# mLSTM in four blocks of 128 tokens with a carried memory, computed with tokens on partitions inside the input projections

## The reference

```
lf = log_sigmoid(fg); bt = cumsum(lf)                       # within a chunk
dmat[t,s] = bt[t] - bt[s] + ig[s]   (s <= t)
mt  = max(max_s dmat, bt + m)
w   = exp(dmat - mt);  sqk = (q k^T / sqrt(128)) * w
num = sqk @ v + exp(bt + m - mt) * (C q);  den = sum(sqk) + exp(bt + m - mt) * (n q)
h   = num / max(|den|, exp(-mt))
C, n = decayed C, n + sum_s wk[s] v[s] k[s]^T, ... k[s]      # memory and normaliser
out_a = rms(sigmoid(o) * h) per head, then times mix_g, then W_out
```

## Time and profile before

| | |
|---|---|
| median of 3 runs | 1237.59 us |
| profiled execution, whole time | 1238.54 us |
| its span in the trace | 1236.7 us |
| TensorE busy in the span | 1164.5 us (94%) |
| VectorE / ScalarE / GpSimd busy | 534.4 / 339.7 / 128.1 us |
| granted clock of TensorE, mean | 0.943 |

### The profile page before, as it was taken

How to read it: one execution, slowest core, us unless ns; L and a number is a source line. 1 busy time by engine, 2 the same in 40 slices (tenths; PEclk the granted TensorE clock), 3 DMA queues, 4 the chain that set the end, 5 groups by cost and what they waited for, 6 DMA issues and landing times.

```text
span 1236.7 us, 21696 instructions
## 1 busy us (share of the span) xinstructions
PE 1164.5 (94%) x9019; PEld 1125.6 (91%) x9019; DVE 534.4 (43%) x820; ACT 339.7 (27%) x426; POOL 128.1 (10%) x231
## 2 busy tenths in 40 slices
PE   6899999999999789999978999889999999999994
PEld 6899999999999779989965779879999999999994
DVE  5435334333334577733743233474333343333345
ACT  5322132221323343122530001243221222212231
POOL 0000709500000006001223100000000000000000
PEclk9999999999999889999986668979999999999997
DMA  5222222332222202221500002212222222322221
GB/s 211 76 93 86 85 86 85 87 94 91 70 93 69 91 35 69 86 69 52 130 28 32 21 17 94 86 33 77 95 85 85 86 85 86 90 94 87 76 76 72
DMA packets 30475, 97.86 MB, mean 79 GB/s; under 512 B 5848, under 2 KB 6104, under 8 KB 30296
## 3 DMA queue, kind: packets, MB, share of 16 engines
q1 hardware_dynamic: 30424, 97.14, 25.0%
HBM read 92.43 MB, written 4.70 MB: 79 GB/s over the span
## 4 chain that ended last, share of the span: by engine, by line
PE 88%; DVE 7%; ACT 2%; DMA 2%; issue 1%; DVEq 0%; SPq 0%; ACTq 0%
PE ps L1471 77%; PE ps L1561 2%; PE ps L1759 1%; DVE y L852 1%; DVE x L856 1%; DMA raw<-wout 1%; PE ps L1766 1%; PE ps L1713 1%; PE ps L1540 1%; DVE xl L805 1%; DVE wl L688 1%; PE ps L1752 1%; ACT wh L402 1%; PE ps L1739 0%; DMA raw<-w 0%
## 5 line engine op out<-in xcount | busy, mean ns | idle before, releaser
L1471 PE MATMUL ps<-xh,wh 128*128 128x272 f32 x1936 | 411.8, 295 | 31.7 <-DVE xl L805 24.5
L688 DVE TENSOR_TENSOR wl<-raw,wh 128x1024 fp32r<-128x1024 f32 (+1 forms) x169 | 205.5, 1216 | 515.3 <-ACT wh L402 514.6
L1471 PE MATMUL ps<-xl,wh 128*128 128x272 f32 x1936 | 406.6, 292 | 0.0
L1471 PE MATMUL ps<-xh,wl 128*128 128x272 f32 x1936 | 404.7, 291 | 0.0
L1471 PEld LDWEIGHTS ps<-xh,wh 128*128 128x128 f32 x1936 | 309.1, 192 | 37.8 <-issue 27.6
L1471 PEld LDWEIGHTS ps<-xl,wh 128*128 128x128 f32 x1936 | 311.1, 193 | 0.0
L1471 PEld LDWEIGHTS ps<-xh,wl 128*128 128x128 f32 x1936 | 309.8, 192 | 0.0
L402 ACT CAST wh<-raw 128x1024 fp32r<-128x1024 f32 (+1 forms) x169 | 173.9, 1029 | 485.4 <-PE ps L1471 476.5
L1471 PE MATMUL ps<-hh,wh 128*128 128x272 f32 x704 | 146.3, 289 | 0.5 <-DVE hl L703 0.5
L1471 PE MATMUL ps<-hl,wh 128*128 128x272 f32 x704 | 145.3, 288 | 0.0
L1471 PE MATMUL ps<-hh,wl 128*128 128x272 f32 x704 | 145.3, 288 | 0.0
(11 more groups left out here) (359 smaller groups left out, 711.1 us busy)
## 6 DMA issues: line engine op xcount, KB each, us to landing
raw<-w SPq DMA_DIRECT2D x120, 512.0 KB, 3.5
raw<-win SPq DMA_DIRECT2D x25, 512.0 KB, 3.5
raw<-w SPq DMA_DIRECT2D x16, 384.0 KB, 3.1
raw<-wout SPq DMA_DIRECT2D x8, 512.0 KB, 3.8
x<-xT SPq DMA_DIRECT2D x4, 544.0 KB, 6.7
o_yT<-x SPq DMA_DIRECT2D x8, 272.0 KB, 2.0
cs<-cT SPq DMA_DIRECT2D x1, 2048.0 KB, 8.1
o_sC<-cs SPq DMA_DIRECT2D x4, 512.0 KB, 2.6
```

Source lines behind the costliest of these rows:

```text
L688: V.tensor_tensor(wl[par][:, 0:cols], raw[par][:, 0:cols], wh[par][:, 0:cols].bitcast(F32), ALU.subtract).then_inc(split_done, 1)
L1471: last = mm(ps[:, bank + s, 0:HALF], w[par][:, kk * P:(kk + 1) * P], a[:, kk, s * HALF:(s + 1) * HALF], start=(kk == 0 and i == 0), stop=( ...
```

## The change

The mLSTM works in four blocks of 128 prompt tokens; between blocks a memory of 128 x 129 floats per head (the normaliser is its column 129, since a column of ones is added to v) is decayed and added to. Only the diagonal 128 x 128 blocks of scores are computed; earlier tokens come in through `q` (scaled by the carried decay) times the memory. Numerators and denominators come out with tokens on partitions, 129 columns per head, so that a head's norm is a sum along the free axis on VectorE, and the scaled result is turned back by TensorE (`turn_cat`). The samples' 32 tokens of four heads fill 128 partitions as one more block. The output gate `o` is turned to tokens on partitions too (`turn_o`). GpSimd no longer masks the weights; the mask is a large number added in the exponent.

The input projection's order becomes gates, u, k, q, v, o, convolution, and nearly all of this work stands in `after` behind units 8 and 13 to 23. The four memory loads (516 KB each) stand behind the weight loads of units 16 to 19, and the stores of memories and of the convolution's state behind weight loads of the output projection. The output projection reads its tiles in the order S5, heads, convolution; its first two units are interleaved by these groups (`out_tiles`). The samples' new memory is computed behind output units 2 to 4 (`sample_memory`).

```diff
 MIX_BASE = FFN_UNITS
 OUT_BASE = MIX_BASE + M_END
...
+                if 16 <= i < 16 + MH:
                     spe.wait_ge(ys_evac, 1)
-                    spe.dma_start(cs[:], A["cT"]).then_inc(cs_in, 16)
+                    spe.dma_start(cs[:, i - 16], A["cT"][:, i - 16]).then_inc(cs_in, 16)
...
                 load(OUT_BASE + m, (OUT_BASE + m) % 2, A["wout"][m])
+            spe.wait_ge(c_ready, NT)
+            store(A["o_pC"], pst[:])
+            spe.wait_ge(cps_used, 3)
+            for h in range(MH):
+                store(A["o_sC"][:, h], cs[:, h])
...
+            def memory(a):
+                dve.wait_ge(st_done, a + 1)
+                dst = cst4[:, a] if a < NT - 1 else pst[:]
+                if a == 0:
+                    note(V.tensor_copy(two(dst), blocks(4)))
+                else:
+                    dve.wait_ge(msc_exp, 1)
+                    for h in range(MH):
+                        src = ps[:, 4 + h // 2, (h % 2) * (P + 1):(h % 2 + 1) * (P + 1)]
+                        note(V.scalar_tensor_tensor(dst[:, h], cst4[:, a - 1, h], step[:, h, a - 1:a], src, ALU.mult, ALU.add))
+                settle()
+                V.memset(stat[:, 52:53], 0.0).then_inc(c_ready, 1)
+            def head_var(a, bank, n):
+                dve.wait_ge(num_done, n + 1)
+                if a < NT:
+                    dve.wait_ge(so_ready, MH + 1)
+                    note(V.tensor_tensor(two(so[:, a]), blocks(bank)[:, :, :, 0:P], two(so[:, a]), ALU.mult))
+                    den = hden[:, a]
+                    note(V.tensor_copy(den.rearrange("p (b h) -> p b h", b=2), blocks(bank)[:, :, :, P]))
+                    emt, tiles = cols[:, 2, a], [so[:, a, h] for h in range(MH)]
+                else:
+                    dve.wait_ge(so_ready, MH + 1)
+                    note(V.tensor_tensor(so_s[:], ps[:, bank, 0:P], so_s[:], ALU.mult))
+                    den = hden[:, NT, 0:1]
+                    note(V.tensor_copy(den, ps[:, bank, P:P + 1]))
+                    emt, tiles = sgc[:, 2:3], [so_s[:]]
+                settle()
+                V.memset(stat[:, 52:53], 0.0).then_inc(on_ready, 1)
+                note(V.scalar_tensor_tensor(den, den, -1.0, den, ALU.mult, ALU.max))
+                for h, t in enumerate(tiles):
+                    note(V.tensor_tensor_reduce(scr[:, h], t, t, 1.0 / DH, 0.0, ALU.mult, ALU.add, hsq[:, a, h:h + 1]))
+                settle()
+                w = len(tiles)
+                link(V.tensor_tensor(den, den, emt, ALU.max))
+                link(V.tensor_tensor(den, den, den, ALU.mult))
+                V.scalar_tensor_tensor(hvar[:, a, 0:w], den, EPS, hsq[:, a, 0:w], ALU.mult, ALU.add).then_inc(hvar_ready, 1)
...
+            def head_cat(a, n):
+                dve.wait_ge(hstd_ready, n + 1)
+                if a < NT:
+                    link(V.reciprocal(hvar[:, a], hvar[:, a]))
+                    V.tensor_tensor(so[:, a], so[:, a], hvar[:, a].unsqueeze(2).to_broadcast([P, MH, P]), ALU.mult)\
+                        .then_inc(cat_ready, 1)
+                else:
+                    link(V.reciprocal(hvar[:, a, 0:1], hvar[:, a, 0:1]))
+                    V.tensor_scalar(so_s[:], so_s[:], hvar[:, a, 0:1], None, ALU.mult).then_inc(cat_ready, 1)
...
+                if s in (21, 22):
+                    memory(s - 21)
+                if s == 22:
+                    side_sum()
+                if s == 23:
+                    head_var(0, 6, 0)
+                    memory(2)
                 if s in (M_HC + 2, M_HC + 3):
                     conv_in(s - M_HC - 2)
+                if s == 24:
+                    scale_col(7, S5_G * S5_CH, wait_bc=False)
+                    head_var(NT, 6, 2)
+                    head_cat(0, 0)
+                    head_var(1, 4, 1)
+                if s == 25:
+                    dve.wait_ge(bc_done, cnt["norm"])
+                    side_scaled(0, gl[:, 0], 4, 5)
+                    side_scaled(1, gl[:, 1], 4, 5)
+                    head_cat(NT, 1)
+                    head_cat(1, 2)
+                    side_low(0, gl[:, 0])
+                    side_low(1, gl[:, 1])
                 if s in (M_BG + 2, M_BG + 3):
                     conv_out(s - M_BG - 2)
...
+                if s == 25:
+                    head_var(2, 6, 3)
+            cat_low(0, 0, 6)
+            cat_low(1, 1, 7)
+            head_cat(2, 3)
+            side_sum()
+            cat_low(2, 2, 6)
+            head_var(3, 4, 4)
+            scale_col(7, D_CONV, wait_bc=False)
+            head_cat(3, 4)
+            memory(3)
+            cat_low(3, 3, 5)
+            cat_low(4, NT, 4)
+            dve.wait_ge(bc_done, cnt["norm"])
+            side_scaled(2, cg[:, 0], 7, 6)
+            side_scaled(3, cg[:, 1], 7, 6)
+            side_low(2, cg[:, 0])
+            side_low(3, cg[:, 1])
...
+            pool.wait_ge(ot_done, MH + 1)
+            pool.wait_ge(ps_ready, 1)
+            settle()
+            note(G.tensor_tensor(vbig[:], vns[:].unsqueeze(1).to_broadcast([P, DEC_BATCH, P + 1]),
+                                 wkb[:].unsqueeze(2).to_broadcast([P, DEC_BATCH, P + 1]), ALU.mult))
+            signal(vw_ready)
+            pool.wait_ge(num_done, 3)
             for h in range(MH):
...
                 note(G.tensor_tensor(cs[:, h], cs[:, h],
-                                     sbc[:, h, DEC_SEQ - 1::DEC_SEQ].unsqueeze(2).to_broadcast([P, DEC_BATCH, P]), ALU.mult))
-                signal(cdec_ready)
+                                     sbc[:, h, DEC_SEQ - 1::DEC_SEQ].unsqueeze(2).to_broadcast([P, DEC_BATCH, P + 1]), ALU.mult))
+            signal(cdec_ready)
...
+            def scores(a):
+                pe.wait_ge(kw_ready, MH) if a < 2 else pe.wait_ge(p_ready, a - 1)
+                for h in range(MH):
+                    t = slice(a * P, (a + 1) * P)
+                    ins = mm(ps[:, 4 + a % 2, h * P:(h + 1) * P], k[:, h, t], q[:, h, t], start=True, stop=True)
+                ins.then_inc(sc_done, 1)
...
+            def memory(a):
+                if a == 0:
+                    pe.wait_ge(glu_sig, 2)
+                else:
+                    pe.wait_ge(c_ready, a)
+                pe.wait_ge(kw_ready, MH)
+                pe.wait_ge(vn_ready, MH)
                 for h in range(MH):
-                    ins = nc.tensor.transpose(ps[0:TS, 7, h * P:(h + 1) * P], v[:, h, SEQ:], ident)
-                ins.then_inc(nat_done, 1)
-            after = {3: [sample_bu], 4: [s5_chunks], 12: [s5_y, s5_y_sample], 14: [gate_spread], 15: [gate_turn],
-                     16: [lambda: glu(0)], 17: [lambda: glu(1)], 21: [lambda: turn(0)], 22: [lambda: turn(1)],
-                     23: [lambda: turn(2)], 24: [lambda: turn(3), turn_sample]}
+                    ins = mm(ps[:, 4 + h // 2, (h % 2) * (P + 1):(h % 2 + 1) * (P + 1)], kw[:, a, h], vn[:, a, h], start=True, stop=True)
+                ins.then_inc(st_done, 1)
...
+            def numerators(a, bank):
+                pe.wait_ge(p_ready, a + 1)
+                if a == 0:
+                    pe.wait_ge(so_ready, MH)
+                else:
+                    pe.wait_ge(c_ready, NT - 1)
+                    pe.wait_ge(q_scaled, 1)
+                if a == 2:
+                    pe.wait_ge(on_ready, 2)
+                for h in range(MH):
+                    out = ps[:, bank + h // 2, (h % 2) * (P + 1):(h % 2 + 1) * (P + 1)]
+                    ins = mm(out, wgt[:, a, h], vn[:, a, h], start=True, stop=(a == 0))
+                    if a:
+                        ins = mm(out, q[:, h, a * P:(a + 1) * P], cst4[:, a - 1, h], start=False, stop=True)
+                ins.then_inc(num_done, 1)
+            def numerators_sample():
+                pe.wait_ge(on_ready, 1)
+                pe.wait_ge(ps_ready, 1)
+                pe.wait_ge(qs_ready, 1)
+                pe.wait_ge(cs_in, 16 * MH)
+                for h in range(MH):
+                    r = slice(32 * h, 32 * h + 32)
+                    mm(ps[r, 6, 0:P + 1], wgt_s[r], vns[r], start=True, stop=False, skip_group_check=True)
+                for b in range(DEC_BATCH):
+                    for h in range(MH):
+                        at = 256 * h + TS * b
+                        ins = mm(ps[32 * h:32 * h + 32, 6, 0:P + 1], qsd[:, at:at + TS], cs[:, h, b], start=False,
+                                 stop=(b == DEC_BATCH - 1), skip_group_check=True)
+                ins.then_inc(num_done, 1)
...
+            def turn_cat(n, a, bank):
+                pe.wait_ge(cat_ready, n + 1)
+                if a < NT:
+                    for h in range(MH):
+                        ins = nc.tensor.transpose(ps[:, bank, h * P:(h + 1) * P], so[:, a, h], ident)
+                else:
+                    ins = nc.tensor.transpose(ps[:, bank, 0:P], so_s[:], ident)
+                ins.then_inc(ct_done, 1)
...
+            after = {3: [sample_bu], 4: [s5_chunks], 8: [gate_turn], 12: [s5_y, s5_y_sample], 13: [gate_spread],
```

(118 more changed lines are left out.)

708 lines of the change are left out of this document (343 added, 365 removed).

## The result

The changed kernel takes 1168.04 us (median of 4 runs, 1166.31 to 1170.88), the kernel before 1239.51 beside it: ratio 0.942, 95% interval 0.939 to 0.945. The profiled execution took 1168.33 us with a span of 1166.4. Forecast were 1171 us and a range of 1159 to 1187.

The account below looks back on a forecast made before the run. TensorE, busy 94% of the span, was taken as the bound. The output units were to end at 730.2 instead of 796.9, a gain of 66.7 us, taking 1238.54 to 1171.8, stated as 1171 us; range 1159 to 1187.

Parts of the forecast that it names:

- TensorE to unit 21: Input projection's units with inserted heads' work: TensorE sets the pace without waits, unit 21 ending at 618.5 us.
- The spread and its unit: Spreading the running maximum on TensorE: 4.64 us, and 2.3 us more for the input unit behind it.
- Unit 24: Last input unit on TensorE: ends at about 647 us, where it ended near 627.5 before.
- Case E: Heads' part between input units: TensorE waits for VectorE's carried memory, +2 to +4 us; chance 0.51 together with the forecast.
- VectorE's closing stage: From unit 21's end to the heads' tiles: VectorE sets the pace, 54.4 us plus 6.0 for GpSimd's decays, ready at 679.
- The sum of squares: In `head_var` on VectorE: 0.45 us taken for each, between 0.24 and 0.95.
- The collisions: GpSimd's four memory decays stretch VectorE's operations beside them: 6.0 us, between 0 and 7.6.
- Behind the heads' tiles: Output projection from 679: first two units 12.4 us, weights 0.9, six units and samples' memory 37.9, ending at 730.2.
- A: Rival: VectorE's work before the output projection is cheaper (fewer collisions, cheaper sums of squares, overlapped convolution), 1163 us; chance 0.20.
- B: Rival: that VectorE work is dearer, 17 sums of squares at 0.95 us and round trips at half clock, 1183; chance 0.14.
- D: Rival: TensorE's clock stays low from unit 14 on, +92 us against a gain of 66.7, 1263 us; chance 0.02.
- C: Rival: TensorE's clock falls behind every insertion after units 14 to 20, +14 us, 1185 us; chance 0.11.

Follow-up runs that it names:

- the experiment: Changed kernel with GpSimd's four decays of the samples' memory held back until the side path's low parts are written: 1162.26 us, ratio 0.937.

## Why the prediction was right, step by step

- **TensorE to unit 21** was forecast to end at 618.5 and ends at 618.2, without a wait. S5 8.4 as forecast. The gates cost 2.9 + 2.9 for a forecast 4.4; by luck what stands ahead of them ended 1.4 us earlier in this trace (in the second trace of the same code 1.9 us later). The spread and its unit cost 5.1 + 1.9 for 4.6 + 2.3. Scores, turnings and GLU came at their prices (1.98 for eight scores, 0.235 each forecast at 1.88; GLU 3.7 for 4.0).
- **Unit 24** ends at 652.3, not 647: TensorE waits 3.62 us for VectorE's `on_ready` at 641.49, and has a clock of 0.64 in the 4.7 us behind it. Case E had waits for the carried memory between units; none came. This wait is another, for a PSUM bank that `head_var` must have read, behind unit 23, where the time is VectorE's. From 652.3 to 672.0 TensorE is busy for 11.1 of 19.7 us, more than the half that was forecast. TensorE in order of time there (start, us, the wait ahead in brackets):

```profile
641.49 0.46 PE L1909 MATMUL ps<-vn,wgt 128*128 128x129 f32 x2 [3.62 <-DVE stat L1242]
```

- **VectorE's closing stage** was the step whose size was off: 60.4 us forecast, 53.8 measured. The sum of squares costs 0.28 + 0.08 us busy, overlapping to a pitch of 0.21, where 0.45 was taken, with 0.24 as its lower bound: 17 x (0.45 - 0.21) = 4.1 us. Even the bound was too high. The rest, 2.5, is spread over small operations. The collisions were 6.6 by their rows and 6.0 by the experiment, for 6.0.
- **Behind the heads' tiles** the forecast was 12.4 + 0.9 + 37.9 = 51.2 us; it was 53.3: the first three full units took 6.2 us instead of 6.03 and the three memory parts 2.4 for 1.7 (39.3 for 37.9 in all), and the first two units 14.0 for 13.3. The clock at the start was 0.59.
- **Sum**: the output units end 4.9 us earlier than forecast (725.3 for 730.2), a gain of 71.6 there; the span fell by 70.3. The closing stage alone was 6.6 us off; that the sum is 4.9 off owes 2.1 to the opposite miss behind it.

Of the rivals, A (a cheaper stage) is half true: its sums of squares were cheaper than even it had them, but the collisions came in full. B and D are refuted by the rows above (0.21 us; clock 1.00 over 57 us). C is wrong for turnings and scores, which is what it was about; what it cites from the earlier trace rows, lower clock behind work with 4 rows of the array, came at the two places where the forecast already had it. What the prediction did not separate is where the gain comes from: it spoke of cover to fill, and 55 of 75 us (1241.4 to 1166.5 on one chip) come without the place between the input units.

## What to carry to other kernels

Before crediting overlap, build the moved work unmoved: here its new form, with what stayed beside it, gave nearly three times what its place between the units gave. Once TensorE's stream is full, find the step from which another engine sets the pace (double an operation before it and behind it), and look which engine's side work starts exactly there: one wait that delayed four GpSimd operations gave 6 us. A long DMA piece in the chain may hold its instruction for only a small part of its length; look at when the instruction could have started without it, and at what the next one waits for, before pricing it.

## What was unexpected of the hardware

- Behind or within matmuls of 4 rows and 512 columns TensorE's granted clock fell to its lower level in six of eight traces, though the engine never waited; the same columns over 128 rows, mostly zero, kept it at 1.00 in each of four (doubled: 16.5 against 12.9 us for eight of them and a unit).
- A product with an accumulated column over 128 x 128 has a pitch of 0.21 us, less than a `scalar_tensor_tensor` of 128 columns without one (L1161, the exponents: 4.20 for 16, 0.26 each).
- A VectorE operation of 32 columns beside GpSimd's lasts as long as GpSimd's: 1.91 us in place of 0.18.
